# Three blocks of a modulation product moved behind the first half's state products, and u's read-back asked for ahead of the blocks' loads

## The chip, the cores and the metric

The kernel runs on one core of a Trainium2 chip, in float32. The metric is the device time of one execution in microseconds, as the median of several runs. TensorE multiplies, VectorE, ScalarE and GpSimd work element by element, and SyncE issues most of the DMAs, in one fixed order, waiting on semaphores where a buffer or an operand isn't ready.

## What is computed

One layer of a diffusion backbone on 256 latent tokens and 256 context tokens of width 1024, cut to what matters here:

```
mod_x = silu(c) @ w_mod + b_mod        # 1024 x 6144: shift1, scale1, gate1, shift2, scale2, gate2
mod_c = silu(c_ctx) @ w_mod + b_mod
hx = modulate(rmsnorm(x), shift1, scale1);   hc = the same of the context
ux = hx @ w_in;   uc = hc @ w_in[:, 512:]
states = bidirectional complex-diagonal scan of u[:, 512:], context first
ssm_x = gelu(C h + D u) * sigmoid(... @ w_glu)
pool_x = pooling mixer of ux[:, :512]
x = x + gate1 * (concat(pool_x, ssm_x) @ w_out)
h2 = modulate(rmsnorm(x), shift2, scale2)
x = x + gate2 * moe(h2)                # 32 experts, 1024 -> 512 -> 1024, top 2 of a routed group
out = rmsnorm(x)
```

## The kernel before

w_mod is used in three thirds of 2048 columns. The first third (shift1, scale1) is multiplied early. The second third (gate1, shift2) is loaded in eight blocks of 128 rows, 1 MB each, into three buffers in turn, and TensorE multiplies block k with the silu'd conditioning columns (`mod_chunk(1, k, 6)`, lines 503 and 511, all into PSUM bank 6). ScalarE then copies the sum to `modrow` (L983). The last third (scale2, gate2) is summed on VectorE (`mod_sum`) out of parts that `last_third` loads.

The scan is a matter of matrices. `u_ssm(q)` (L612) makes four groups of u. ScalarE evacuates each (L1015) and sends it to a scratch tensor in DRAM (L1018). SyncE reads it back in another layout, `U8`, in two halves of eight DMAs (L305), each half when both of its groups are out (`u_out0`, `u_out1`). `state_inputs(h)` (L644) multiplies the half's `U8` into four PSUM groups, n = 4h to 4h + 3. Group 2 also waits for `mo_ready`, since its bank holds operands of the tables that VectorE is making (`table`, L1179 and L1267). `turn_kernels` (L600) transposes the convolution kernels; ScalarE copies them and issues 15 Toeplitz copies (L1046, L1047), five ahead of the second half's states and ten behind them. VectorE scans the states, which ends in `hp_ready`.

`u_pool(t)` (L625) is the pooling half of the input projection, then come windows (L677), pooling weights (L683), the Toeplitz product (L692), the pooling part of the output projection (`mix_pool`, L699, which needs the `wo_pool` weights), the states' outputs (L715), the GLU (L737), the last third's row sums (L749, L750), the SSM part of the output projection (L790), the routing, and the loop over groups of four experts (L824 to L894).

TensorE's order and SyncE's order are both written out by hand. Every SyncE request stands behind the ones before it: w_mod blocks of the second third (L289), w_out in two parts (L315 `wo_ssm`, L319 `wo_pool`), the parts of the last third (L294), w_glu (L325), expert weights (L243, L250). A block's load waits on `mod_used`, a count of the blocks multiplied, for its buffer.

Of the kernel before, what the change touches and what calls it, by code (L numbers as in the profile page):

```python
# [58 lines left out]
def hybrid_block(nc, x, ctx, w_mod, columns, ssm_bc, b_mod_rows, w_in, w_out, w_pool, w_glu, w_router, b_router,  # L59
                 w_gate, w_up, w_down, g_final, consts, pool_consts, out):  # L60
    D = x.shape[2]
    KD = D // P
# [11 lines left out]
    with ExitStack() as stack:  # L74
# [5 lines left out]
        def S(name):  # L80
            if name not in sems:
                sems[name] = stack.enter_context(nc.semaphore(name))
            return sems[name]
# [181 lines left out]
        def _(sp):  # L265
# [35 lines left out]
            for h in range(2):  # L301
                sp.wait_ge(S(f"u_out{h}"), 16 * 2)
                at = slice(128 * h, 128 * h + 128)
                for s in range(L):
                    sp.dma_start(ra[SG * s:SG * (s + 1), 0:2048].rearrange("i (g n) -> i g n", g=8)[:, :, at],  # L305
                                 u_dram.rearrange("(g i) (s n) -> s i g n", g=8, s=L)[s][:, :, at]).then_inc(S(f"u8_in{h}"), 16)
                for k in range(3 + 3 * h, min(6 + 3 * h, KD)):
                    mod_chunk(1, k)
                if h == 0:
                    sp.wait_ge(S("mo_powers"), 1)  # L310
                    sp.wait_ge(S("pw_ready"), 1)
                    sp.dma_start(wpool, w_pool[0].rearrange("g c d -> c g d")).then_inc(S("wpool_in"), 16)
# [182 lines left out]
        def _(pe):  # L495
# [127 lines left out]
            def u_pool(t):  # L623
                for k in range(KD):
                    mm = pe.matmul(ps[:, t, :], hT[:, k, 256 + P * t:256 + P * t + P], WBp[:, k, :],  # L625
                                   start=(k == 0), stop=(k == KD - 1))
                mm.then_inc(S("u_pool_mm"), 1)
# [23 lines left out]
            pe.wait_ge(S("win_ssm_in"), 16)  # L651
            u_ssm(0)
            u_ssm(1)
            pe.wait_ge(S("ks_copy"), 1)
            for k in range(3):
                mod_chunk(1, k, 6)
            u_ssm(2)
            u_ssm(3)
            pe.wait_ge(S("st_copy"), 16)
            state_inputs(0)  # L660
            turn_kernels()
            for k in range(3, 6):
                mod_chunk(1, k, 6)
            state_inputs(1)
            for k in range(6, KD):
                mod_chunk(1, k, 6)
            pe.wait_ge(S("kt_ready"), 2)
            pe.wait_ge(S("win_pool_in"), 16)
            u_pool(0)
            u_pool(1)  # L670

            pe.wait_ge(S("pmat_in"), 16)
# [947 lines left out]
```

## Time and profile before

| | us |
|---|---|
| median of 3 runs | 660.44 |
| lowest, highest | 660.02, 662.47 |
| profiled execution | 657.66 |
| its span | 655.8 |
| TensorE busy | 589.1 (90%) |
| VectorE busy | 202.2 (31%) |
| ScalarE busy | 146.9 (22%) |

The page of the profile cuts the span into 40 slices of 16.4 us and gives the busy share of each engine, the clock granted to TensorE and what the DMA engines moved. Of the chain that ended last, 70% is TensorE and 24% DMA. The timeline gives merged instructions in order of time, with idle time ahead of them and what ended it.

### The profile page before, as it was taken

The numbers are of one execution on the slowest core, as the hardware profiler recorded it, in microseconds if no ns is written. First come the engines' busy times: TensorE is split into PE (matmuls) and PEld (weight loads), VectorE is DVE, ScalarE is ACT, GpSimd is POOL, SyncE is SP. The second block draws the span as 40 slices with busy tenths as digits, with TensorE's granted clock in tenths as the row PEclk, the third lists the DMA queues.
The fourth block names the chain that finished last, engine by engine and source line by source line (L and its number), as shares of the span: only waits on it lengthen the run. The fifth ranks groups of instructions, "written<-read, shape, count | busy, mean of one in ns | idle before, by whom it ended". The sixth has DMA issues, their size and how long they took to land.

```text
span 655.8 us, 9396 instructions
## 1 busy us (share of the span) xinstructions
PE 589.1 (90%) x3778; PEld 248.8 (38%) x3778; DVE 202.2 (31%) x434; ACT 146.9 (22%) x231; POOL 52.1 (8%) x99
## 2 busy tenths in 40 slices
PE   1999969999979997899799789979997997999995
PEld 0454544564543342334233323423342342334331
DVE  7999679968830020011001000200200010002003
ACT  8551321131232122102121301221022112012111
POOL 4994000000010000000000000000000000000000
PEclk9999979999999998999799989989998999899998
DMA  8994799998989999999999999999999999999951
GB/s 323 420 399 120 254 319 337 410 408 320 364 321 416 420 420 423 423 421 420 423 423 423 419 423 422 424 419 422 423 423 419 422 423 423 422 420 375 404 233 64
DMA packets 47463, 248.99 MB, mean 380 GB/s; under 512 B 8888, under 2 KB 11592, under 8 KB 21072
## 3 DMA queue, kind: packets, MB, share of 16 engines
q1 hardware_dynamic: 41224, 243.93, 91.6%
q10 hardware_dynamic: 5864, 3.68, 2.1%
q0 software_dynamic: 352, 1.07, 0.7%
q8 instruction: 15, 0.25, 0.2%
q14 instruction: 8, 0.07, 0.0%
HBM read 244.46 MB, written 2.11 MB: 376 GB/s over the span
## 4 chain that ended last, share of the span: by engine, by line
PE 70%; DMA 24%; DVE 2%; SPq 1%; issue 1%; ACT 1%; DVEq 0%; POOL 0%
PE ps L854 24%; DMA wts<-in_w_up 17%; PE ps L894 17%; PE ps L830 5%; PE ps L824 5%; PE ps L612 4%; DMA wts<-in_w_in 3%; PE ps L699 2%; PE ps L625 2%; PE ps L790 2%; DMA wts<-in_w_mod 2%; PE ps L870 1%; PE ps L737 1%; PE ps L511 1%; PE ps L644 1%
## 5 line engine op out<-in xcount | busy, mean ns | idle before, releaser
L854 PE MATMUL ps<-wts,ra 128*64 128x512 f32 x512 | 241.8, 625 | 34.2 <-DMA wts<-in_w_up 31.3
L855 PE MATMUL ps<-wts,ra 128*64 128x512 f32 x512 | 241.9, 626 | 0.0
L854 PEld LDWEIGHTS ps<-wts,ra 128*64 128x64 f32 x512 | 70.0, 143 | 179.6 <-issue 136.3
L894 PE MATMUL ps<-wts,ra 128*32 128x512 f32 x512 | 111.4, 593 | 0.0
L894 PE MATMUL ps<-rc,ra 128*32 128x512 f32 x512 | 111.4, 593 | 0.0
L1179 DVE TENSOR_TENSOR ra<-ra,ps 128x256 f32<-128x256 f32 x32 | 13.5, 421 | 267.9 <-ACT ra L1128 267.8
L1122 ACT COPY ra<-ps 128x512 f32<-128x512 f32 x32 | 33.6, 1050 | 208.9 <-PE ps L855 208.9
L855 PEld LDWEIGHTS ps<-wts,ra 128*64 128x64 f32 x512 | 70.0, 143 | 0.0
L894 PEld LDWEIGHTS ps<-wts,ra 128*32 128x32 f32 x512 | 29.1, 110 | 73.2 <-issue 73.2
L1179 DVE TENSOR_TENSOR cb<-ps,ra 128x512 f32<-128x512 f32 x32 | 22.1, 691 | 103.4 <-PE ps L894 103.4
L1117 ACT COPY ra<-ps 128x512 f32<-128x512 f32 x32 | 18.7, 585 | 133.2 <-PE ps L824 133.2
L483 POOL TENSOR_SCALAR small<-small 128x1 f32<-128x1 f32 x4 | 0.7, 186 | 473.4 <-ACT ra L1160 465.1
L824 PEld LDWEIGHTS ps<-cb,ra 128*128 128x128 f32 x256 | 29.8, 191 | 13.4 <-issue 6.5
L824 PE MATMUL ps<-cb,ra 128*128 128x128 f32 x256 | 32.8, 281 | 0.9 <-ACT ra L1111 0.9
L830 PE MATMUL ps<-cb 128*128 128x512 f32 x68 | 32.9, 606 | 0.0
L612 PE MATMUL ps<-ra,wts 128*128 128x512 f32 x64 | 29.4, 599 | 1.4 <-DMA wts<-in_w_in 1.0
L894 PEld LDWEIGHTS ps<-rc,ra 128*32 128x32 f32 x512 | 29.2, 110 | 0.0
L1179 DVE TENSOR_TENSOR cb<-cst,ut 128x256 f32<-128x256 f32 x16 | 6.7, 420 | 46.0 <-PE ps L824 44.8
L870 PEld LDWEIGHTS ps<-cst,ra 128*128 128x128 f32 x128 | 14.2, 141 | 17.2 <-issue 15.3
L511 PE MATMUL ps<-wts,sil 128*32 128x512 f32 x96 | 13.2, 637 | 7.7 <-DMA wts<-in_w_mod 7.7
L870 PE MATMUL ps<-cst,ra 128*128 128x128 f32 x128 | 18.8, 280 | 0.0
L830 PEld LDWEIGHTS ps<-cb 128*128 128x128 f32 x68 | 11.6, 190 | 15.5 <-issue 14.6
(228 smaller groups left out, 533.1 us busy)
## 6 DMA issues: line engine op xcount, KB each, us to landing
wts<-in_w_up SPq DMA_DIRECT2D x64, 1024.0 KB, 15.5
wts<-in_w_gate SPq DMA_DIRECT2D x64, 1024.0 KB, 13.4
wts<-in_w_down SPq DMA_DIRECT2D x30, 1024.0 KB, 9.8
rc<-in_w_down SPq DMA_DIRECT2D x30, 1024.0 KB, 12.5
wts<-in_w_mod SPq DMA_DIRECT2D x16, 1024.0 KB, 14.9
r<-in_w_mod SPq DMA_DIRECT2D x6, 1024.0 KB, 14.1
wts<-in_w_in SPq DMA_DIRECT2D x2, 2048.0 KB, 23.2
wts<-in_w_out SPq DMA_DIRECT2D x2, 2048.0 KB, 17.0
```

The source lines that it names most:

```text
L511: mm = pe.matmul(ps[32 * j:32 * j + 32, bank, :], silc[:, k, :], w[:, 512 * j:512 * j + 512], start=False, stop=(k == KD - 1))
L612: mm = pe.matmul(ps[:, 4 + q % 2, :], WBs[:, k, P * q:P * q + P], hT[:, k, :], start=(k == 0), stop=(k == KD - 1))
L625: mm = pe.matmul(ps[:, t, :], hT[:, k, 256 + P * t:256 + P * t + P], WBp[:, k, :], start=(k == 0), stop=(k == KD - 1))
L824: mm = pe.matmul(o, h2P[:, t, k, :], Pm[:, t], start=True, stop=True, skip_group_check=True)
L830: mm = pe.matmul(ps[:, 2 * t + h, :], PT[:, t, :], oS[:, 2 * h + t, :], start=False, stop=stop, skip_group_check=True)
L854: pe.matmul(ps[0:64, 4 + b, :], st, Wg[b][:, k, :], start=(k == 0), stop=(k == KD - 1))
L855: mm = pe.matmul(ps[64:128, 4 + b, :], st, Wu[b][:, k, :], start=(k == 0), stop=(k == KD - 1))
L870: mm = pe.transpose(ps[:, 6 + j % 2, P * f:P * f + P], gu[:, j % 2, P * f:P * f + P], ident)
L894: mm = pe.matmul(ps[32 * j:32 * j + 32, BANKS[n], :], hid[:, j, f, SLOTS * t:SLOTS * t + SLOTS], Wd[j][:, f, 512 * h:512 * h + 512], start ...
L1117: act.copy(xm[:, 2 * r:2 * r + 2], ps[:, GATHER[r], :].rearrange("p (k e s) -> p k e s", k=2, e=4)).then_inc(S("xm_ready"), 1)
L1122: act.copy(gu[:, j % 2, :].rearrange("p (f q) -> p q f", f=FC), ps[:, 4 + j % 2, :].rearrange("p (q f) -> p q f", f=FC)).then_inc(S("gu_co ...
L1179: return dve.tensor_tensor(o, a, b, op)
```

## The change

On SyncE, the loads of blocks 3 to 5 of the second third move from behind the first half's read-back to behind the second half's, together with 6 and 7. On TensorE, blocks 0 to 2 move from between u_ssm(1) and u_ssm(2) to behind the first half's states and the kernels' transposes; blocks 3 to 5 move behind the second half's states; blocks 6 and 7 move between u_pool(0) and u_pool(1).

```diff
                                  u_dram.rearrange("(g i) (s n) -> s i g n", g=8, s=L)[s][:, :, at]).then_inc(S(f"u8_in{h}"), 16)
-                for k in range(3 + 3 * h, min(6 + 3 * h, KD)):
+                for k in range(3 * h, KD * h):
                     mod_chunk(1, k)
...
             u_ssm(0)
             u_ssm(1)
-            pe.wait_ge(S("ks_copy"), 1)
-            for k in range(3):
-                mod_chunk(1, k, 6)
             u_ssm(2)
             u_ssm(3)
             pe.wait_ge(S("st_copy"), 16)
             state_inputs(0)
             turn_kernels()
-            for k in range(3, 6):
+            pe.wait_ge(S("ks_copy"), 1)
+            for k in range(3):
                 mod_chunk(1, k, 6)
             state_inputs(1)
-            for k in range(6, KD):
+            for k in range(3, 6):
                 mod_chunk(1, k, 6)
             pe.wait_ge(S("kt_ready"), 2)
             pe.wait_ge(S("win_pool_in"), 16)
             u_pool(0)
+            for k in range(6, KD):
+                mod_chunk(1, k, 6)
             u_pool(1)
```

TensorE behind `u_ssm(1)`, before: the bias (L503) and three blocks (L511, `r` and `wts` being the buffers) stand ahead of the two u groups that are left (L612).

```order
L612 MATMUL ps<-ra,wts 128x512 x2
L503 MATMUL ps<-mr,cst 32x512 [waits bmod_in,ks_copy]
L503 MATMUL ps<-mr,cst 32x512 x3
L511 MATMUL ps<-r,sil 32x512 [waits wmod_in2]
L511 MATMUL ps<-r,sil 32x512 x3
L511 MATMUL ps<-wts,sil 32x512 [waits wmod_in0]
L511 MATMUL ps<-wts,sil 32x512 x3
L511 MATMUL ps<-wts,sil 32x512 [waits wmod_in1]
L511 MATMUL ps<-wts,sil 32x512 x3
L612 MATMUL ps<-ra,wts 128x512 [waits u_ssm_ev]
L612 MATMUL ps<-ra,wts 128x512 x7
```

TensorE at the same place, after: u follows at once, and the first half's states (L644) behind it.

```order
L612 MATMUL ps<-ra,wts 128x512 x2
L612 MATMUL ps<-ra,wts 128x512 [waits u_ssm_ev]
L612 MATMUL ps<-ra,wts 128x512 x7
L612 MATMUL ps<-ra,wts 128x512 [waits u_ssm_ev]
L612 MATMUL ps<-ra,wts 128x512 x7
L644 MATMUL ps<-ra,wts 64x64 [waits u_ssm_ev,u8_in0,st_copy]
L644 MATMUL ps<-ra,wts 64x64 x15
L644 MATMUL ps<-ra,wts 64x64 [waits u_ssm_ev]
L644 MATMUL ps<-ra,wts 64x64 x15
L644 MATMUL ps<-ra,wts 64x64 [waits mo_ready]
L644 MATMUL ps<-ra,wts 64x64 x15
```

So the first half's states, their wait for `mo_ready` among them, come earlier by the bias and three blocks.

TensorE behind the last group of the second half's states, after: three blocks, u_pool(0), two blocks, u_pool(1). Before, only the two blocks of buffers 2 and 0 stood there, ahead of both u_pool.

```order
L644 MATMUL ps<-ra,wts 64x64 x15
L511 MATMUL ps<-r,sil 32x512 [waits wmod_in2]
L511 MATMUL ps<-r,sil 32x512 x3
L511 MATMUL ps<-wts,sil 32x512 [waits wmod_in0]
L511 MATMUL ps<-wts,sil 32x512 x3
L511 MATMUL ps<-wts,sil 32x512 [waits wmod_in1]
L511 MATMUL ps<-wts,sil 32x512 x3
L625 MATMUL ps<-wts,ra 128x512 [waits win_pool_in,kt_ready]
L625 MATMUL ps<-wts,ra 128x512 x7
L511 MATMUL ps<-r,sil 32x512 [waits wmod_in2]
L511 MATMUL ps<-r,sil 32x512 x3
```

The work of eight blocks is as before; five of them now stand behind the second half's states instead of two.

SyncE between the two read-backs, the difference (three block loads leave the place ahead of w_pool and the second read-back):

```order
 L305 DMA ra<-u_scratch 16x8x128 [waits u_out0]
 L305 DMA ra<-u_scratch 16x8x128 x7
-L289 DMA r<-in_w_mod 128x2048 [waits mod_used]
-L289 DMA wts<-in_w_mod 128x2048 [waits mod_used] x2
 L312 DMA lam<-in_w_pool 128x4x128 [waits pw_ready,mo_powers]
 L305 DMA ra<-u_scratch 16x8x128 [waits u_out1]
 L305 DMA ra<-u_scratch 16x8x128 x7
+L289 DMA r<-in_w_mod 128x2048 [waits mod_used]
+L289 DMA wts<-in_w_mod 128x2048 [waits mod_used] x2
 L289 DMA r<-in_w_mod 128x2048 [waits mod_used]
 L289 DMA wts<-in_w_mod 128x2048 [waits mod_used]
```

All five blocks, 3 to 7, are now asked for behind the second read-back, and w_out's two parts behind them.

## Rows read from the trace of the kernel before

**Rows 1.** Page, section 2: what the DMA engines moved, in 40 slices of 16.4 us

```profile
GB/s 323 420 399 120 254 319 337 410 408 320 364 321 416 420 420 423 423 421 420 423 423 423 419 423 422 424 419 422 423 423 419 422 423 423 422 420 375 404 233 64
```

**Rows 2.** Chain of waits: start us, us, what

```profile
77.01 4.30 DMA u_scratch<-ut
...
85.00 4.75 DMA ra<-u_scratch
...
119.73 7.06 PE ps L699 x16
...
185.83 0.64 PE ps L854
...
254.35 18.88 DMA wts<-in_w_up
```

**Rows 3.** TensorE timeline, 40 to 120 us: start us, us, instruction, idle before

```profile
58.60 1.06 PE L503 MATMUL ps<-mr,cst 1*32 1x512 f32 x8
...
62.30 14.00 PE L612 MATMUL ps<-ra,wts 128*128 128x512 f32 x32
76.23 3.95 PE L644 MATMUL ps<-ra,wts 128*64 128x64 f32 x128
80.11 1.09 PE L600 MATMUL ps<-cst,cb 128*128 128x128 f32 x8
...
89.79 6.32 PE L644 MATMUL ps<-ra,wts 128*64 128x64 f32 x128 [5.88 <-DMA ra<-u_scratch]
...
97.90 14.00 PE L625 MATMUL ps<-wts,ra 128*128 128x512 f32 x32
```

**Rows 4.** Windows of 1 us: length, busy per engine, TensorE's granted clock, DMA share, GB/s

```profile
88.00:89.00 1.00, 0.00 (x0) 0.00 (x0) 0.93 (x4) 0.00 (x0) 0.00 (x0) 0.62 1.25 246
...
95.00:96.00 1.00, 1.00 (x36) 0.98 (x32) 0.00 (x0) 0.77 (x2) 0.00 (x0) 0.97 1.04 410
```

**Rows 5.** VectorE timeline: last table, first gate sum, gated products

```profile
75.32 1.22 DVE L1267 SCALAR_TENSOR_TENSOR rc<-rc,ps 128x1024 f32<-128x1024 f32 x1
...
143.89 0.75 DVE L1387 TENSOR_SCALAR cb<-wts,sil 128x1024 f32<-128x1024 f32 x1
...
148.72 2.00 DVE L1179 TENSOR_TENSOR wts<-rc 128x256 f32<-128x256 f32 x4
```

**Rows 6.** SyncE: timeline row of a read-back; waits for expert weights' requests (in total, times, longest)

```profile
62.26 3.65 SPq L305 DMA_DIRECT2D ra<-u_scratch  x8
...
SPq L243 <- PE ps L855: 237.4, 60, 10.2
```

**Rows 7.** DMA queues (packets, MB, engine share): q10 over 84 to 88, q1 over 120 to 156

```profile
q10 hardware_dynamic: 356, 0.60, 73.3%
...
q1 hardware_dynamic: 3160, 14.86, 101.9%
```

**Rows 8.** One request each, issue start us, then its landing: wo_pool, blocks 3, 6, last gate's first

```profile
L319 SPq DMA_DIRECT2D wts<-in_w_out x1: 368/368/368, 96.2 to 96.2; - x1
...
DMA to landing us min/median/max: 18.8/18.8/18.8
...
L289 SPq DMA_DIRECT2D r<-in_w_mod x1: 428/428/428, 66.0 to 66.0; - x1
...
DMA to landing us min/median/max: 5.5/5.5/5.5
...
L289 SPq DMA_DIRECT2D r<-in_w_mod x1: 529/529/529, 85.7 to 85.7; - x1
...
DMA to landing us min/median/max: 6.5/6.5/6.5
...
L294 SPq DMA_DIRECT2D wts<-in_w_mod x1: 378/378/378, 128.3 to 128.3; - x1
...
DMA to landing us min/median/max: 13.4/13.4/13.4
```

**Rows 9.** TensorE timeline, 120 to 200 us: SSM part of the output projection

```profile
152.40 12.18 PE L790 MATMUL ps<-wts 128*128 128x512 f32 x28
```

## The prediction

> **What bounds the kernel now.** I read the chain of waits first, then the TensorE timeline of the stretch that the diff touches, then what the DMA queue does there. The second half of the kernel is the expert loop. Its passes wait for expert weights (such a step of the chain is 18.9 us long), and the slices of the page carry 420 GB/s from there to the end [rows 1, 2]. The requests for those weights wait for TensorE's own gate and up products [rows 6], so the stream cannot start before the loop does, at 185.83 [rows 2]. A microsecond won or lost ahead of 185.83 is a microsecond at the end. The change lies at 58 to 112 us, so the question is what it does to 185.83.
>
> In the stretch, TensorE multiplies three w_mod blocks at 58.60 to 62.30 while u of the last two groups is still owed. That u then goes out to DRAM and back (write 4.30, read back 4.75 behind its last issue), and TensorE stands idle for 5.88 us ahead of the second half's states at 89.79 [rows 2, 3]. The idle costs twice. The granted clock is 0.62 at 88 to 89 us and is back at 0.97 at 95 to 96, so it went from the 2.4 GHz level to the 1.2 GHz level after some 4.7 us of standing, and the 128 state matmuls behind it took 6.32 us where the same 128 of the first half took 3.95 [rows 3, 4]. From 97.9 on TensorE has work almost without a gap until it reaches the output projection at 119.73 [rows 2, 3].
>
> **The change on TensorE.** Bias and three blocks are worth 62.30 - 58.60 = 3.70 us; leaving them out there ends u_ssm(3) at 76.23 - 3.70 = 72.5. The first half's four state groups are 3.88 us (76.23 to 80.11), 0.97 each [rows 3]. Groups 0 and 1 run to 74.5. Group 2 waits for mo_ready, which VectorE gives behind a table that ends at 75.32 + 1.22 = 76.54 [rows 5]; before, TensorE came to that wait at 78.2 and never felt it. So 2.0 us of new idle, states done at 78.5, the kernels' transposes (1.03) at 79.6, bias and blocks 0 to 2 at 81.5, 82.4 and 83.3.
>
> u of the second half: evacuated and sent at 73.2, written by 77.5 if the write stays at 4.30, eight reads issued over 3.65 us [rows 6], landed at 85.5 if the last takes 4.75 again. No w_mod block moves beside it now, so it will be sooner; I take 83.3, no wait, with 85.5 as the late end. At full clock the states are then done at 87.2. If nothing else were in the way the gain would be 5.88 - 2.0 = 3.9 us of idle and 6.32 - 3.95 = 2.4 of clock, 6.3 in all.
>
> **What is late next: blocks 3 to 5.** SyncE asked for them at 66 us, in a stretch in which the DMA engines had room (254 GB/s in that slice) [rows 1, 8]. Now the requests stand behind the reads of u and each needs the buffer of block 0, 1 or 2, so they go out at 81.6 to 83.4. A block on an idle queue landed 5.5 us after its issue, so block 3 lands at 87.2. In a full queue q1 moved 14.86 MB in 36 us, 2.53 us for a block of 1.049 MB [rows 7, 8]. That gives 89.7 and 92.2 for blocks 4 and 5. Beside them run the Toeplitz copies that ScalarE issues: its first five took 73.3% of the engines over 84 to 88, 2.9 us, and some more at the edges, 3.7 at most [rows 7]. They start about 1.5 us sooner now (their releaser, the kernels' transposes, is that much earlier), so part of them is over before block 3's data come. I take 1.6 us, bounds 0 and 3.7. Block 5 lands at 93.8 (92.2 to 95.9), TensorE is through with it at 94.8, and has waited three times for about 1.6 us on the way.
>
> Then u_pool(0), 7.0 us (half of the 14.00), blocks 6 and 7 (1.9 together, asked for behind blocks 3 and 4, and landed 5 to 8 us behind block 5, under the 7.0), u_pool(1): 110.7, where before it ended at 111.9. TensorE would stand ready for the output projection at 119.73 - 1.2 = 118.5 (116.9 to 120.6).
>
> **The weights of the output projection.** wo_pool was asked for at 96.2 and landed 18.8 later, at 115.0, with 4.7 us to spare [rows 8]. The six MB between block 6 (85.7 + 6.5 = 92.2) and wo_pool took 22.8 us where a clear queue needs 15.2; the other 7.6 are the later ten Toeplitz copies and their small packets. Now the queue holds ten MB in a row: block 3 at 87.2 + 1.6, then four blocks, wo_ssm 2, the first gate part 1 and wo_pool 2, nine times 2.53 = 22.8, and the same 7.6: 119.2 (117.6 to 121.3). The issue gates don't break this row: each next request is released by a block that lands before the ones ahead of it are through. So the weights come 4.2 us later than before, eat the 4.7 to spare, and the projection starts at 119.2 to 119.4 where it started at 119.73: **-0.4 us** (-2.1 to +1.6). The gain of 6.3 is almost all taken back by 3 MB that used to move in a free stretch.
>
> hp_ready doesn't decide: before, TensorE came to it at 119.73 + 7.06 = 126.8 and went on at once; VectorE's work on the second half starts with its states, some 5 us sooner now, and TensorE comes at about 126.4. SyncE's waits for blocks 6 and 7 now stand in front of wglu's request, but that is released by u_pool(1), which is later on TensorE than both.
>
> **Behind it.** The queue stays 4.2 us late until it runs empty near 156 us. Of what lands in it, one thing is near its use: the first part of the last gate, 128.3 + 13.4 = 141.7, used by VectorE at 143.89 [rows 5, 8]. At 145.9 VectorE is 2.0 late, its four gated products start at 150.7 instead of 148.72 and end at 152.7. TensorE comes for them at 152.4 and takes 0.86 us for each where VectorE takes 0.5 [rows 5, 9], so it waits for none, but VectorE is a few tenths late for its next step. I put 0 to 0.6 on it, **+0.3**.
>
> **Sum** against the profiled execution's own 657.66 (span 655.8): -0.4 + 0.3 = -0.1, 657.6. The median of the runs shown is 660.44, 2.8 above that execution, so the same sum gives **660.3**. The bounds -2.1 and +2.2 give 658.3 and 662.6.
>
> **Rivals.**
> *The loads come in time (faster).* If the first five Toeplitz copies are through before block 3's data, block 5 lands at 92.2 and wo_pool at 117.6; TensorE is ready at 116.9. The projection starts 2.1 us sooner, VectorE's gate parts are only 2.6 us late: 658.3. For it: nothing moves at 80 to 82 us except those copies. Against: they were strung over 6 us before. To be over 0.5% faster (3.3 us) the ten later copies would have to cost less than 7.6 as well. Chance 0.21, of that 0.05 for more than 3.3.
> *The clock falls again (slower).* TensorE has bursts of 0.95 us between waits of 1.6 from 87 to 94. If that is enough for the 1.2 GHz level to be granted for as long as before (about 6.8 us, from the change inside 88 to 89 to the one inside 95 to 96 [rows 4]), it falls on u_pool(0) and half of it is lost, 3.4 us: ready at 121.9, +2.2 and 0.3 more behind, 662.9. It decides as soon as it costs over 0.7 us, since the weights are only that much later than TensorE. Against: the one fall in this stretch came after 4.7 us without a single matmul, and the gaps here are a third of that, 1.6 each. Chance 0.13. The Trainium skill speaks for it: "TensorE: Matmul & The Clock Gate", section on HAM oscillation, describes a kernel whose short bursts between DMA waits are thrown back to half clock at every wait. By that rule this rival would be the likeliest; but the waits it describes are 3 to 5 us long, and the trace agrees only for the long one.
> *The queue is later than I take it (slower).* All 3.7 us of Toeplitz work fall on the blocks: wo_pool lands at 121.3, +1.6; the gate part is 4.1 late, the products end near 154.8, and VectorE's next step carries 0.9 of it: +2.5, 662.9. It decides from a tax of 2.1 us on. Chance 0.13. The Trainium skill's "DMA: Bandwidth & Descriptors", rules for kernel authors, says to issue a DMA early and wait for it late; the change does the opposite for three blocks. By that rule alone one would expect the loss; the trace agrees in so far as slice 66 to 82 had room that is now unused [rows 1].
> *The idle isn't filled as the change says.* If u still lands at 85.5, the states end at 89.4, and block 5 at 93.8 is met later with less waiting. 94.8 stays. This falls together with the forecast.
>
> **How the numbers follow.** Forecast 0.50, loads in time 0.21, clock 0.13, late queue 0.13, anything else 0.03. The range takes in the rivals' times and about half a us at each end for the spread of the runs: 657.8 to 663.3. A measurement of this kernel can tell about 0.5%, 3.3 us. Over 3.3 faster: 0.05, and 0.01 of the rest. Over 3.3 slower: where the clock and the full tax come together (120.6 + 3.4 = 124.0, +4.3), 0.06, and 0.01 of the rest. Within: 0.87.
>
> **What the profile after would show.** Right: the 5.88 us idle ahead of the second states is gone or under 2 us; a new idle of about 2 us inside the first states, released by VectorE; states of the second half in some 4 us at clock 1.00; two or three idles ahead of blocks 3 to 5, released by DMA, 3 to 6 us in all; wo_pool landing at 118 to 121 with a wait of TensorE ahead of the output projection; expert loop starting within 1 us of 185.83. Wrong: no wait for blocks 3 to 5 (then the Toeplitz term is too big), clock below 1 anywhere in 88 to 103 (the second rival), or the loop starting more than 2 us away from 185.83 although wo_pool landed near 119.

## The result, and the profile after

| | before | after |
|---|---|---|
| median, us (20 runs each) | 660.82 | 664.04 |
| lowest, highest | 659.21, 665.3 | 659.87, 667.2 |
| profiled execution, its span | 657.66, 655.8 | 663.57, 661.8 |
| output projection's first matmul | 119.73 | 125.11 |
| expert loop's first matmul | 185.83 | 189.59 |

The ratio is 1.004 [1.0022, 1.0057]: the change makes the kernel slower by about 2.6 us (3.2 by the medians). That is outside the forecast's range, on the side of the slower rivals, and less than the 3.3 us that the prediction took as the least it could tell. Of all the executions below one, of experiment 2, was in a slower state (668.33 us); the ratios leave it out.

The DMA slices of the page after, to be laid beside [rows 1]:

```profile
GB/s 315 418 401 118 92 312 345 407 414 403 354 297 408 422 420 422 422 419 424 421 422 421 423 421 422 422 422 422 423 421 422 422 422 422 421 421 366 408 229 63
```

The fifth slice, 66 to 82 us, carried 254 GB/s before and carries 92 now. That is the 3 MB which moved out of it. The three slices behind it, into which the loads moved, carry the same as before within 3%: there was no room in them for more.

TensorE's timeline of the stretch (start us, us, instruction, idle before and what ended it), to be laid beside [rows 3]:

```profile
72.78 2.09 PE L644 MATMUL ps<-ra,wts 128*64 128x64 f32 x64
76.88 2.64 PE L644 MATMUL ps<-ra,wts 128*64 128x64 f32 x64 [2.01 <-DVEq L1302]
79.45 1.97 PE L600 MATMUL ps<-cst,cb 128*128 128x128 f32 x8
...
85.14 3.95 PE L644 MATMUL ps<-ra,wts 128*64 128x64 f32 x128
89.25 1.06 PE L511 MATMUL ps<-r,sil 128*32 128x512 f32 x8 [0.15 <-DMA r<-in_w_mod]
94.83 1.59 PE L511 MATMUL ps<-wts,sil 128*32 128x512 f32 x8 [4.52 <-DMA wts<-in_w_mod]
98.56 1.93 PE L511 MATMUL ps<-wts,sil 128*32 128x512 f32 x8 [2.13 <-DMA wts<-in_w_mod]
100.42 7.93 PE L625 MATMUL ps<-wts,ra 128*128 128x512 f32 x16
...
110.14 7.13 PE L625 MATMUL ps<-wts,ra 128*128 128x512 f32 x16
...
125.04 7.13 PE L699 MATMUL ps<-wts 128*128 128x512 f32 x16
```

The 5.88 us of idle ahead of the second half's states are gone, and these take 3.95 us instead of 6.32, as the change intends. In their place stand 2.01 us ahead of group 2 and 0.15, 4.52 and 2.13 ahead of blocks 3 to 5. The idle total is no smaller than before (8.8 us against 5.88). Two groups are also slow for their size: the 64 state matmuls at 76.88 take 2.64 us where the 64 ahead of them took 2.09, and the kernels' transposes (L600) 1.97 instead of 1.09.

The clock says why. Windows of 2 us of the kernel after: the column behind POOL is TensorE's granted clock, then DMA share and GB/s.

```profile
78.00:80.00 2.00, 2.00 (x37) 1.88 (x33) 0.00 (x0) 1.51 (x4) 0.00 (x0) 0.54 0.39 102
80.00:82.00 2.00, 2.00 (x15) 1.21 (x13) 1.29 (x4) 1.14 (x4) 0.00 (x0) 0.60 0.35 102
...
94.00:96.00 2.00, 1.17 (x8) 0.16 (x8) 1.93 (x7) 0.00 (x0) 0.00 (x0) 0.81 0.99 327
96.00:98.00 2.00, 0.42 (x4) 0.00 (x0) 1.97 (x7) 0.00 (x0) 0.00 (x0) 0.50 1.03 341
...
100.00:102.00 2.00, 2.00 (x6) 0.84 (x3) 1.93 (x9) 0.00 (x0) 0.00 (x0) 0.50 1.09 298
102.00:104.00 2.00, 2.00 (x6) 0.86 (x5) 1.83 (x11) 0.00 (x0) 0.00 (x0) 0.98 0.99 320
```

TensorE went from its 2.4 GHz level to the 1.2 GHz level soon behind the 2.01 us at mo_ready (the idle ends at 76.88, the clock is 1.00 up to 78), and again behind the 4.52 us ahead of block 4. It is at half speed over most of 78 to 82 and of 95 to 102.

SyncE's timeline shows the requests:

```profile
76.44 4.84 SPq L305 DMA_DIRECT2D ra<-u_scratch  x8
83.56 0.35 SPq L289 DMA_DIRECT2D r<-in_w_mod  x1
84.41 1.19 SPq L289 DMA_DIRECT2D wts<-in_w_mod  x2
```

| block | asked for | landed | forecast for the landing |
|---|---|---|---|
| 3 | 83.56 | 89.2 | 88.8 |
| 4 | 84.4 | 94.8 | 91.3 (89.7 + 1.6) |
| 5 | 85.3 | 98.5 | 93.8 |

The DMA queues over 84 to 88 and 92 to 96 us (packets, MB, share of the 16 engines); q1 carries SyncE's loads, q10 ScalarE's Toeplitz copies:

```profile
q1 hardware_dynamic: 126, 1.02, 84.4%
q10 hardware_dynamic: 132, 0.20, 16.1%
...
q1 hardware_dynamic: 149, 1.08, 80.4%
q10 hardware_dynamic: 147, 0.25, 20.4%
```

While the copies run, q1 brings 1.02 MB in 4 us, 0.26 MB/us, where [rows 7] has 0.41. All 15 copies were issued before block 5 had landed: five over 82.6 to 85.1, ten over 89.2 to 95.6.

The chain that ended last runs through the load of block 5, and not through wo_pool (start us, us, what):

```profile
85.27 13.24 DMA wts<-in_w_mod
98.56 1.93 PE ps L511 x8
...
125.11 7.06 PE ps L699 x16
```

wo_pool was asked for at 101.0 and landed 21.2 us later, at 122.2. That is later than forecast (119.2, at most 121.3), but 2.9 us ahead of its use. The load of block 5 and TensorE's work behind it decided.

### The profile page after: what moved, and what is told of

Same layout as the page of the kernel before. It is cut to its first block, busy times and chain, and to the rows that moved or that the text cites. A ratio compares the mean times of both kernels' runs of the same rounds, so it can differ in the third digit from the quotient of the medians.

```text
span 661.8 us, 9396 instructions
## 1 busy us (share of the span) xinstructions
PE 592.2 (89%) x3778; PEld 248.2 (38%) x3778; DVE 202.5 (31%) x434; ACT 147.0 (22%) x231; POOL 52.0 (8%) x99
## 3 DMA queue, kind: packets, MB, share of 16 engines
q10 hardware_dynamic: 5864, 3.68, 2.0%
q0 software_dynamic: 352, 1.07, 0.7%
## 4 chain that ended last, share of the span: by engine, by line
PE 63%; DMA 22%; DVE 11%; issue 1%; SPq 1%; ACT 0%; DVEq 0%; POOL 0%
PE ps L854 23%; DMA wts<-in_w_up 19%; PE ps L894 17%; PE ps L830 5%; PE ps L824 4%; DVE rc L1179 4%; DVE ps L1179 3%; PE ps L625 2%; PE ps L699 2%; PE ps L790 2%; DMA wts<-in_w_mod 2%; DMA cb<-in_ssm_bc 1%; PE ps L870 1%; PE ps L737 1%; PE ps L511 1%
## 5 line engine op out<-in xcount | busy, mean ns | idle before, releaser
L612 PE MATMUL ps<-ra,wts 128*128 128x512 f32 x64 | 29.1, 597 | 1.4 <-DMA wts<-in_w_in 1.0
L511 PE MATMUL ps<-wts,sil 128*32 128x512 f32 x96 | 14.8, 701 | 14.9 <-DMA wts<-in_w_mod 14.8
```

The source lines that it names most:

```text
L511: mm = pe.matmul(ps[32 * j:32 * j + 32, bank, :], silc[:, k, :], w[:, 512 * j:512 * j + 512], start=False, stop=(k == KD - 1))
L612: mm = pe.matmul(ps[:, 4 + q % 2, :], WBs[:, k, P * q:P * q + P], hT[:, k, :], start=(k == 0), stop=(k == KD - 1))
```

## The experiments

All are set against runs of the kernel before on the same chip. The medians of before were 660.92 (29 runs; experiments 1 to 4), 661.24 (23 runs; 5 to 8) and 660.67 (29 runs; 9 to 11). Times at which TensorE starts a group are those of its timeline, in which the projection starts at 119.66 in before and at 125.04 in after. Each kernel has one trace, so such a time is one execution's.

**1. Blocks behind u_pool.** The SyncE order of the change is kept, and TensorE has 7 us of other work while blocks 3 to 5 come. ScalarE's copy of the sum goes behind its two copies of u (those lines are left out here).

```diff
             state_inputs(1)
-            for k in range(3, 6):
-                mod_chunk(1, k, 6)
...
             u_pool(0)
-            for k in range(6, KD):
+            for k in range(3, 6):
                 mod_chunk(1, k, 6)
             u_pool(1)
+            for k in range(6, KD):
+                mod_chunk(1, k, 6)
```

> The changed kernel, but TensorE takes blocks 3 to 5 only behind u_pool(0) and blocks 6 and 7 behind u_pool(1) (ScalarE copies the sum and sends it behind its two copies of u). No load is asked for earlier than in the changed kernel. Theory A, the late loads of blocks 3 to 5 hold TensorE: its 6.8 us of waits ahead of u_pool(0) vanish, u_pool(0) starts near 89 instead of 100.4; what is late next is wo_pool, which landed at 122.2 in the changed kernel and still does at 120 to 124, so TensorE then waits for it and the output projection starts at 120 to 123 instead of 125.1: 660 to 663. Theory B, the queue behind block 5 doesn't matter and only TensorE's path did: the projection starts at 114, some 11 us sooner, 653. Theory C, it is the granted clock that was lost and not the blocks: the clock falls at the wait for mo_ready as before, and the time stays near 664.

Measured: 662.28, ratio 1.0012 [0.9985, 1.0039]. TensorE's timeline:

```profile
76.82 3.55 PE L644 MATMUL ps<-ra,wts 128*64 128x64 f32 x64 [2.26 <-DVEq L1301]
...
88.90 7.13 PE L625 MATMUL ps<-wts,ra 128*128 128x512 f32 x16
...
99.05 1.07 PE L511 MATMUL ps<-wts,sil 128*32 128x512 f32 x8 [1.16 <-DMA wts<-in_w_mod]
...
121.16 8.75 PE L699 MATMUL ps<-wts 128*128 128x512 f32 x16 [4.88 <-DMA wts<-in_w_out]
```

The three waits of 6.8 us shrink to 1.16, TensorE is ready for the projection at 116.3, and then it stands 4.88 us for wo_pool. So the late blocks are what puts the projection at 125 in after, and behind them the full queue holds this cure at 121. The clock falls again behind the 2.26 us at mo_ready (3.55 us for 64 matmuls) and behind the 4.88 us (8.75 us for the 16 matmuls of the projection, 7.13 in before).

**2. Blocks 0 to 2 inside the mo_ready wait.**

```diff
                     elif n == 2:
+                        pe.wait_ge(S("ks_copy"), 1)
+                        for k in range(3):
+                            mod_chunk(1, k, 6)
                         pe.wait_ge(S("mo_ready"), 1)
```

> The changed kernel with blocks 0 to 2 between the second and the third group of the first half's states, where TensorE stood idle for 2.0 us on mo_ready. The idle vanishes and the clock shouldn't fall at 78; blocks 0 to 2 end at 78 instead of 85, so that the loads of blocks 3 to 5 go out right behind u's read-back, at 81.3 instead of 83.6 to 86. Theory A: the blocks land about 2 us sooner, block 5 at 96, and the end comes 2 to 3 us sooner than in the changed kernel, 661 to 662. Theory C, clock: the same idle filled gives 1.6 us at full clock, and more if the later falls go too, 660 to 662; the two are told apart by the landings of blocks 4 and 5. If neither, 664.

Measured: 661.4, ratio 1.0004 [0.9981, 1.0028]. The 2.0 us idle is gone, the clock stays at 1.00 there, the requests go out at 80.9 instead of 83.6, block 5 is multiplied at 94.08 and the projection starts 4.5 us sooner than in after:

```profile
90.33 1.07 PE L511 MATMUL ps<-wts,sil 128*32 128x512 f32 x8 [1.46 <-DMA wts<-in_w_mod]
94.08 1.94 PE L511 MATMUL ps<-wts,sil 128*32 128x512 f32 x8 [2.68 <-DMA wts<-in_w_mod]
95.95 7.89 PE L625 MATMUL ps<-wts,ra 128*128 128x512 f32 x16
...
120.52 7.13 PE L699 MATMUL ps<-wts 128*128 128x512 f32 x16
```

Filling that one idle takes back the whole loss that can be measured, but no more: the time can't be told from before's. The late queue is still felt further on. VectorE waits for the last gate's first part, which it did not in before, and TensorE for the gated products behind it:

```profile
146.79 0.75 DVE L1387 TENSOR_SCALAR cb<-wts,sil 128x1024 f32<-128x1024 f32 x1 [3.58 <-DMA wts<-in_w_mod]
```

```profile
152.71 12.26 PE L790 MATMUL ps<-wts 128*128 128x512 f32 x28 [0.91 <-DVE wts L1179]
```

**3. All Toeplitz copies behind block 5.**

```diff
-            toeplitz(range(3))
             take_states(1)
-            toeplitz(range(3, L))
+            act.wait_ge(S("mod_used"), 14)
+            toeplitz(range(L))
```

> The changed kernel, but ScalarE issues all 15 Toeplitz copies behind block 5's product instead of five ahead of and ten behind the second half's states. Theory A1, the Toeplitz copies on the other queue take the engines from blocks 3 to 5: blocks 4 and 5 land 2.5 us apart, at 91.7 and 94.2 instead of 94.8 and 98.5, u_pool(0) starts at 95 instead of 100.4; the copies land by 118 and the projection starts near 120 to 121: 659 to 661. Theory A2, the blocks are late only because they are asked for late, and the copies cost them nothing: landings at 94.8 and 98.5 as before, 664 or more, since the copies themselves now are late.

Measured: 668.2, ratio 1.0092 [1.0059, 1.0126]. TensorE's timeline:

```profile
93.39 1.06 PE L511 MATMUL ps<-wts,sil 128*32 128x512 f32 x8 [2.68 <-DMA wts<-in_w_mod]
94.39 7.13 PE L625 MATMUL ps<-wts,ra 128*128 128x512 f32 x16
...
121.67 3.64 PE L692 MATMUL ps<-wts,ra 128*32 128x128 f32 x64 [5.28 <-DMA wts<-ra]
```

Blocks 3, 4 and 5 land 5.2, 7.3 and 10.2 us behind their requests; in after it was 5.6, 10.4 and 13.2. The copies cost block 5 **3.0 us**. The other 2.1 of the 5.1 by which block 5 is sooner here are the earlier request (83.16 against 85.27). Over 84 to 88 q1 brings 1.61 MB here, 1.02 in after. Even without copies block 5 came 3.7 us behind block 4, not 2.53. Over 90 to 94 us of this run q1 moved 1.25 MB, 0.31 MB/us, with no copies beside it: the rate of 0.41 [rows 7] was not reached here. The kernel as a whole loses, against 659 to 661 expected: the Toeplitz product now waits 5.28 us for its copies and runs at half clock behind that, so the projection starts at 125.24, as in after. What this run loses beyond after lies behind the projection (pauses and clock, see below).

**4. Useless matmuls in the waits.** Extra work on TensorE into PSUM banks that are overwritten later, nothing left out: two in front of the mo_ready wait, five ahead of block 4, two ahead of block 5.

```diff
+            def filler(n, bank):
+                for _ in range(n):
+                    pe.matmul(ps[:, bank, :], ident, cst[:, 0:512], start=True, stop=True)
...
                     elif n == 2:
+                        pe.wait_ge(S("ks_copy"), 1)
+                        filler(2, 6)
                         pe.wait_ge(S("mo_ready"), 1)
...
+            pe.wait_ge(S("kt_ready"), 2)
             mod_chunk(1, 3, 6)
+            filler(5, 0)
             mod_chunk(1, 4, 6)
+            filler(2, 0)
             mod_chunk(1, 5, 6)
```

> The changed kernel with matmuls of no use (128x512 of constants into a PSUM bank that is overwritten later) in its three waits: two ahead of the wait for mo_ready, five ahead of block 4, two ahead of block 5. They keep TensorE busy and change nothing else. Theory C, the granted clock is what was lost: it stays at 1.00 over 76 to 104, states and transposes of 76 to 82 take 1.6 us less, blocks 4, 5 and the start of u_pool(0) 2 us less: 660 to 661. Theory A, the loads: blocks 4 and 5 still land 11 and 14 us behind block 2, only what lies behind block 5 gains, about 1.5 to 2 us: 662 to 663.

Measured: 662.99, ratio 1.0025 [0.9998, 1.0052]. The clock is 1.00 from 76 to 173 us and the projection starts at 122.13:

```profile
97.32 1.07 PE L511 MATMUL ps<-wts,sil 128*32 128x512 f32 x8 [0.48 <-DMA wts<-in_w_mod]
98.31 7.13 PE L625 MATMUL ps<-wts,ra 128*128 128x512 f32 x16
```

So the two clock falls are worth 2.9 of the 5.4 us at the projection: 1.2 because blocks 3 to 5 are asked for and land sooner, 1.7 in the product of block 5 (1.93 to 1.07) and u_pool(0) (7.93 to 7.13). The median fits the 662 to 663 that the theory of the loads gave. It does not show the whole 2.9, and this execution lost more than that again at 173 to 181 (see below).

**5. Blocks 3 and 4 early, in space of their own.** On top of experiment 2, SyncE asks for blocks 3 and 4 once u_ssm is done, ahead of the second read-back, into 16 KB per partition that is free then. The lines that choose the buffers, and the later places of wo_ssm and of the last third's parts, are left out here.

```diff
             for h in range(2):
+                if h == 1:
+                    sp.wait_ge(S("u_ssm_mm"), 4)
+                    mod_chunk(1, 3)
+                    mod_chunk(1, 4)
                 sp.wait_ge(S(f"u_out{h}"), 16 * 2)
```

> As the run with blocks 0 to 2 in the wait for mo_ready, but blocks 3 and 4 get buffers of their own, the space of w_in's SSM columns, which is free when u_ssm(3) is done. They are asked for at 72.5, ahead of the second read-back, in a stretch in which the DMA engines have almost nothing to do; block 5 is asked for behind the read-back, blocks 6 and 7 right behind it. wo_ssm waits for blocks 3 and 4, the parts of the last third for block 7. Theory A, the 3 MB that used to move in a free stretch are what was lost: blocks 3 and 4 land at 78 to 80, TensorE waits for none of the five, u_pool(0) starts near 90, wo_pool lands near 115, and the output projection starts at 115 to 116 against 119.7 of the kernel before: 657 to 658, faster than before. Theory D, once TensorE is early something else (VectorE's scan, the last third's parts) takes the place: 660 to 661.

Measured: 664.54, ratio 1.0056 [1.0035, 1.0076], the opposite of what I expected. The last u group's write, issued at 76.5, is only through at 85.5, and TensorE stands 9.55 us:

```profile
94.10 6.33 PE L657 MATMUL ps<-ra,wts 128*64 128x64 f32 x128 [9.55 <-DMA ra<-u_scratch]
```

That write took 2.9 us in after, 4.30 in before and some 9 us here: 2 MB of blocks stood ahead of its small packets. (This execution was 3.2 us late at the end of u_ssm already; the 9.55 us of idle are not part of that.)

**6. Blocks 6 and 7 between the two u_pool, alone.** The kernel before with only this.

```diff
-            for k in range(6, KD):
-                mod_chunk(1, k, 6)
...
             u_pool(0)
+            for k in range(6, KD):
+                mod_chunk(1, k, 6)
             u_pool(1)
```

> The kernel before with only the last part of the change: blocks 6 and 7 between u_pool(0) and u_pool(1). Loads and everything ahead of the second half's states as before. Both blocks land (92 and 96) before the states end, so TensorE does the same work in another order. All theories of mine: no difference, 660 to 661, and the output projection at 119.7. If this part alone cost something (ScalarE's copy of the sum, the last third's parts that are asked for behind it), it would show as 1 us or more and would have to be taken off the loads' account.

Measured: 660.56, ratio 0.9998 [0.9979, 1.0017], the projection at 119.70. This part of the change costs and brings nothing.

**7. SyncE's old order.** Experiment 2 with blocks 3 to 5 asked for ahead of the second read-back again.

```diff
-                for k in range(3 * h, KD * h):
+                for k in range(3 + 3 * h, min(6 + 3 * h, KD)):
```

> As the run with blocks 0 to 2 in the wait for mo_ready (all other places of TensorE as in the changed kernel), but with SyncE's order of before: blocks 3 to 5 are asked for ahead of the second read-back. Blocks 0 to 2 end at 76.4 to 78.2 there, so the requests go out then, 5 us sooner than behind the read-back, and the read-back's eight requests only from 78.3 on instead of 76.1, beside 3 MB of blocks. Theory A, the place of the requests on SyncE is what costs: blocks 3 to 5 land at 82, 85 and 88 and hold nobody; u lands at 85 to 88 instead of 82.9, the states start 2 to 5 us later, and the two about cancel on TensorE, while wo_pool lands 3 us sooner: 659.5 to 660.5. Rival: the read-back is the longer wait, the idle ahead of the states is back with its fall of the clock, 661 to 662.

Measured: 671.29, ratio 1.0164 [1.0139, 1.0189]. SyncE's and TensorE's timelines:

```profile
80.09 8.32 SPq L305 DMA_DIRECT2D ra<-u_scratch  x8
```

```profile
94.58 5.66 PE L647 MATMUL ps<-ra,wts 128*64 128x64 f32 x128 [13.21 <-DMA ra<-u_scratch]
```

Beside three block loads the eight requests of a read-back take 8.32 us to issue, not 3.65 [rows 6], and TensorE waits 13.2 us. Both readings that I had set out (659.5 to 662) missed this. With blocks 0 to 2 multiplied this late, asking for u first is right, and worth 10 us: 8.0 at the projection (128.52 against 120.52 in experiment 2), the rest behind it. What made the old SyncE order good was the old TensorE order, which let blocks 3 to 5 go at 66 us.

**8. The kernel before with filler.** Five useless matmuls in its wait for u; nothing is left out.

```diff
+            pe.wait_ge(S("kt_ready"), 2)
+            filler(5, 0)
             state_inputs(1)
```

> The kernel before with five matmuls of no use (128x512 of constants into a PSUM bank that is overwritten later) in its 5.88 us wait for u, nothing else changed. Theory C, the clock: it stays at 1.00 over 84 to 96, the second half's states take 3.95 instead of 6.32 us, and the output projection starts at 117.4 instead of 119.7 (wo_pool has landed at 115.0 by then): 658 to 659. Theory D, what follows is held by the queue or VectorE: 660 to 661.

Measured: 660.01, ratio 0.9986 [0.997, 1.0002].

```profile
91.18 3.95 PE L648 MATMUL ps<-ra,wts 128*64 128x64 f32 x128 [1.45 <-DMA ra<-u_scratch]
...
97.48 1.07 PE L511 MATMUL ps<-wts,sil 128*32 128x512 f32 x8 [1.36 <-DMA wts<-in_w_mod]
```

The states take 3.95 us, the 2.4 us of clock are won, and then TensorE waits 1.36 us for block 7, which it did not in before. The projection starts at 120.24. This execution came to the stretch 1.3 us late (its bias of the second third starts at 59.92, before's at 58.60), so from there to the projection it is 60.3 us against 61.1: 0.7 of the 2.4 us arrive. Of the prize that the change is after, little is there to be won, because the loads behind it are nearly as late. That the median is 1.2 us lower is not shown to be more than noise (the interval reaches 1.0002).

**9. Output weights first.** TensorE's orders of 1 and 2 together; on SyncE wo_pool ahead of blocks 6 and 7, wo_ssm behind the last third's first part, and the first expert weights later.

```diff
-            sp.wait_ge(S("u_ssm_mm"), 4)
+            sp.wait_ge(S("s_mm"), 8)
+            sp.dma_start(wo_pool, w_out_v[:, 0:4, :]).then_inc(S("wo_pool_in"), 16)
+            for k in range(6, KD):
+                mod_chunk(1, k)
+            sp.wait_ge(S("mod_used"), 14)
+            last_third(0, 0)
             sp.dma_start(wo_ssm, w_out_v[:, 4:8, :]).then_inc(S("wo_ssm_in"), 16)
-            sp.wait_ge(S("mod_used"), 14)
-            last_third(0, 0)
-            sp.wait_ge(S("s_mm"), 8)
-            sp.dma_start(wo_pool, w_out_v[:, 0:4, :]).then_inc(S("wo_pool_in"), 16)
```

> The version that the runs so far point to. TensorE: blocks 0 to 2 in the wait for mo_ready, blocks 3 to 5 behind u_pool(0), blocks 6 and 7 behind u_pool(1). SyncE: behind the second read-back blocks 3 to 5, then wo_pool at once, then blocks 6 and 7, the first part of the last third, wo_ssm; the first expert's up and second down weights go behind the last third's third part and x instead of ahead of them. The theory (TensorE waits for what stands ahead in the queue, never for its own work): blocks 3 to 5 are there behind u_pool(0), wo_pool lands near 103 to 106, TensorE starts the pooling part of the output projection at 112 to 114 and then waits for VectorE's scan, which ends at 121 to 122, where the kernel before came there at 126.8: 655 to 657, faster than before by 4 to 5 us. Rival: the expert weights that now stand later in the queue are late for the loop, or the ten megabytes ahead of the gates' parts still hold VectorE: 660 or more.

Measured: 662.01, ratio 1.001 [0.9987, 1.0033], as the rival had it (660 or more). The projection starts at 120.91, not at 112 to 114. TensorE was through u_pool(1) at 104.7, and then:

```profile
107.77 1.91 PE L511 MATMUL ps<-r,sil 128*32 128x512 f32 x8 [3.06 <-DMA r<-in_w_mod]
111.33 1.93 PE L511 MATMUL ps<-wts,sil 128*32 128x512 f32 x8 [1.64 <-DMA wts<-in_w_mod]
```

The wait moved from wo_pool to blocks 6 and 7. VectorE shows one more bound behind all this: its copies of the Toeplitz operands wait for the last copy, in this kernel as in after (2.79 us there):

```profile
114.88 0.63 DVE L1366 COPY ra<-wts 128x256 f32<-128x256 f32 x2 [2.95 <-DMA wts<-ra]
```

The scan that follows ends at 125. The pooling part of the projection takes 7.1 us and TensorE needs the scan behind it, so a projection sooner than about 118 would have met VectorE.

**10. The later ten Toeplitz copies behind block 5.** The first five stay.

```diff
             take_states(1)
+            act.wait_ge(S("mod_used"), 14)
             toeplitz(range(3, L))
```

> The changed kernel, with only the later ten Toeplitz copies issued behind block 5's product; the first five stay where they are. It tells which of the two sets delays the blocks. My prediction charged the first five (1.6 us) and put the ten behind block 5. If the ten are what hit blocks 4 and 5, these land 7.5 and 10.5 us behind their issue, as in the run with all fifteen behind (7.3 and 10.2), instead of 10.4 and 13.2, and block 5 is there at 95 to 96. If it was the first five, block 5 stays near 98. The end: the ten copies are late for the Toeplitz product as all fifteen were there, so 665 to 668 either way.

Measured: 663.08, ratio 1.0033 [1.0011, 1.0054].

```profile
76.30 2.09 PE L644 MATMUL ps<-ra,wts 128*64 128x64 f32 x64 [1.67 <-DVEq L1303]
...
92.71 1.94 PE L511 MATMUL ps<-wts,sil 128*32 128x512 f32 x8 [4.14 <-DMA wts<-in_w_mod]
95.63 1.93 PE L511 MATMUL ps<-wts,sil 128*32 128x512 f32 x8 [0.99 <-DMA wts<-in_w_mod]
97.49 9.00 PE L625 MATMUL ps<-wts,ra 128*128 128x512 f32 x16
```

Block 4 lands 10.4 us behind its request, exactly as in after, and block 5 12.4, where it was 13.2 with all copies and 10.2 with none. Of the 3.0 us the first five copies cost 2.2 and the ten 0.8. (Block 5 is multiplied at 95.6, the time that I had expected if the ten were to blame, but because its request went out 2.1 us sooner than in after; only the time from request to landing tells the two apart.) Here the idle at mo_ready is 1.67 us and the clock holds (2.09 us for 64 matmuls); it falls in block 4's wait of 4.14 us. The end was not the 665 to 668 I had expected from a late Toeplitz product: the projection starts at 123.18. It falls once more further on, with TensorE at work all the time (1.91 to 2.00 us busy in each 2 us from 170 to 180). These eight matmuls take 3.68 us in before:

```profile
174.28 6.42 PE L761 MATMUL ps<-rc,cst 128*128 128x512 f32 x8
```

**11. Both cures.** Experiment 2 and useless matmuls ahead of blocks 4 (two) and 5 (three); nothing is left out.

```diff
             mod_chunk(1, 3, 6)
+            filler(2, 0)
             mod_chunk(1, 4, 6)
+            filler(3, 0)
             mod_chunk(1, 5, 6)
```

> The run with blocks 0 to 2 in the wait for mo_ready (661.4, 0.5 us over before), with two and three matmuls of no use ahead of blocks 4 and 5 as well, so that the clock doesn't fall at 94.6 as it did there. It separates what is left of the clock from what is left of the loads. Clock: u_pool(0) takes 7.13 instead of 7.89 us and block 5's product 1.07 instead of 1.94, the output projection starts at 119.0 instead of 120.5, 660 to 661. Loads: TensorE's waits for blocks 4 and 5 are filled, not shorter, and block 5 still lands at 94: nothing below 660.

Measured: 661.81, ratio 1.0015 [0.9997, 1.0033]. The clock is 1.00 up to 181 us, and:

```profile
119.58 7.13 PE L707 MATMUL ps<-wts 128*128 128x512 f32 x16 [0.20 <-DMA wts<-in_w_out]
```

With no clock lost anywhere the projection starts where it starts in before, and wo_pool now is the last to come. That is the balance that the prediction had forecast for the change itself.

## Why the prediction was wrong

**Right.** The idle ahead of the second states went, and they took 3.95 us at full clock. The new wait for mo_ready was 2.01 us (forecast 2.0). u came back in time. Three waits stand ahead of blocks 3 to 5, though longer than forecast (6.8 us; forecast 3 to 6). VectorE waited for its gate part, 1.25 and 0.41 us (forecast 2.0), and TensorE felt nothing of it. Moving blocks 6 and 7 cost nothing (experiment 6). Two of the signs of being wrong that the prediction named came true: the clock was below 1 in 88 to 103, and the loop started 3.8 us from 185.83.

**The step that failed: "Block 5 lands at 93.8 (92.2 to 95.9)".** It landed at 98.5, 4.7 late. Three terms of it were too small, and they add up to it:

| term | forecast | measured | from |
|---|---|---|---|
| request of block 5 | 83.4 | 85.3 (+1.9) | SyncE's timeline |
| Toeplitz tax on block 5 | 1.6 (0 to 3.7) | 3.0 (+1.4) | experiment 3 |
| request to landing without copies | 8.8 (83.4 to 92.2) | 10.2 (+1.4) | experiment 3 |

The first is mostly the clock. I had counted the 2.0 us at mo_ready as idle only, and wrote that short gaps would not bring a fall since "the one fall in this stretch came after 4.7 us without a single matmul". (That reading was off too: the idle began at 89.79 - 5.88 = 83.9, and a mean clock of 0.62 over 88 to 89 puts the fall at 88.2, 4.3 us later.) In the profiled execution of after, the fall came behind 2.01 us. The two state groups behind it took 0.55 us more, the transposes 0.88 and the bias 0.09, 1.5 in all; 0.3 is mo_ready itself, which came at 76.88 and not at 76.54. The requests, which wait for the buffers of blocks 0 to 2, went out 2 us late. This is a stall whose price is paid on another engine. The second is a choice inside a range: the trace had 3.7 as the upper end, and I took 1.6 because part of the copies would be over in time. They weren't: the three issued from 84 us on landed 7.4 to 10.8 us behind their issue, where the same three had taken 3.8 to 4.5 in before. And the price is not their own share of the engines' time (16.1%): beside 0.05 MB/us of q10, q1 fell from 0.40 (experiment 3) to 0.26 MB/us. For the third I used 2.53 us a block, the rate of a queue that had long been full [rows 7]; without copies block 5 still came 3.7 us behind block 4. Why the queue was slower there stays open.

**The clock rival and the late-queue rival came together.** Behind the landing of block 5 the clock cost 0.9 us in its product and 0.8 in u_pool(0). 4.7 + 0.9 + 0.8 = 6.4, and the forecast's 118.5 for TensorE becomes 124.9 (measured 125.0). I had put 0.06 on the two together costing more than 3.3 us, as if one came without the other. They are not independent: a later block makes a longer wait, behind which the clock can fall, and the lower clock behind mo_ready makes a later request. The price of the clock came out near (3.4 us forecast, 2.9 in experiment 4), but that is luck: I had put all of it on u_pool(0), where 0.8 fell; 0.9 fell on block 5's product, and the rest reached the projection by way of the later requests. The rule of the Trainium skill that I had set aside, "TensorE: Matmul & The Clock Gate", section on HAM oscillation, was the better guide: short bursts between DMA waits are thrown back to half clock. The trace after agrees for the wait of 4.52 us ahead of block 4. The 2.01 us at mo_ready are shorter than any wait that the section describes, and there the measurement goes further than the page.

The length of an idle does not decide by itself. Experiments 2 and 3 both wait 2.68 us for block 5: in 2 its product takes 1.94 us and u_pool(0) 7.89, in 3 they take 1.06 and 7.13, at full clock. Ahead of the loop TensorE stands 2.88 us in before and in after; the clock stays at 1.00 in before and falls in after. 1.67 us in experiment 10 left it at 1.00.

**"The weights come at 119.2, and the projection with them."** wo_pool landed at 122.2, 7.2 us later than before (forecast 4.2). From block 5 to wo_pool it was 23.7 us (forecast 25.4), so that stretch was 1.7 shorter than forecast, against 4.7 of lateness ahead of it. The weights were not the bound in after; they were in experiments 1, 7 and 11.

**From 5.4 to 3.8 us, and to 2.6.** The projection starts 5.4 us later than in before, the loop 3.8. Between the projection and the GLU 1.6 us came back. In before, two pauses stand in this stretch, which nothing in the profile but "issue" explains; with them L715 and L727 take 1.6 us more. They are absent in after:

```profile
132.21 1.07 PE L715 MATMUL ps<-rc,ra 64*32 64x128 f32 x54 [0.76 <-issue]
...
138.13 0.60 PE L727 MATMUL ps<-cst,rc 128*128 128x128 f32 x4 [0.36 <-issue]
```

(These lines are of before.) Pauses of 0.4 to 1.8 us stand there in before and in experiments 3, 4, 6, 8 and 11, and none in after and in 1, 2, 5, 7, 9 and 10. Their cause stays open, and with one trace a kernel it isn't shown that they belong to the kernel and not to the execution. So it isn't known how much of the step from 3.8 to 2.6 they are. In the profiled execution of after the loop's first pass ran at half clock for some 3 us (a window of 2 us):

```profile
192.00:194.00 2.00, 2.00 (x8) 0.64 (x6) 0.00 (x0) 0.00 (x0) 0.00 (x0) 0.50 0.67 274
```

The first pass takes 5.28 us here and 3.59 in before, so 1.7 of the 6.0 us by which the two spans differ are this fall. Experiments 6, 8 and 9 have such a fall at 186 to 190 too, and before has not; experiments 6 and 8 keep before's order of the loads, so the fall does not need the change. The spread of after (659.87 to 667.2) goes with the clock: the mean granted clock of the four fastest executions is 0.967 to 0.970, that of the four slowest 0.958 to 0.961. Where in these the clock fell is not known.

**What the rest comes to.** Of the 5.4 us at the projection, 4.5 go when blocks 0 to 2 fill the mo_ready wait (experiment 2: no fall there, requests sooner). The last 0.9 go with the clock behind blocks 4 and 5 (experiment 11). Nothing goes clearly below before's 119.7, since wo_pool, blocks 6 and 7 (experiment 9) and VectorE's scan stand within 2 us of one another there. No version of this order beat the kernel before.

The projection is not the whole story. First matmuls in one execution of each:

| | projection | GLU | loop | GLU to loop |
|---|---|---|---|---|
| before | 119.66 | 141.14 | 185.83 | 44.7 |
| after | 125.04 | 144.89 | 189.59 | 44.7 |
| experiment 2 | 120.52 | 140.37 | 187.97 | 47.6 |
| 4 | 122.13 | 143.51 | 191.62 | 48.1 |
| 8 | 120.24 | 142.26 | 188.60 | 46.3 |
| 9 | 120.91 | 140.76 | 185.47 | 44.7 |
| 10 | 123.18 | 143.03 | 191.05 | 48.0 |
| 11 | 119.58 | 141.35 | 186.18 | 44.8 |

Where the last column is above 44.8, the clock fell somewhere in 172 to 186 us with at most 0.1 us of TensorE idle ahead of it, and cost 1.7 us (experiments 2 and 8) or 3.4 (4 and 10; about as much in 3 and 7). In experiment 2, 0.9 us more is the wait for the gated products. The prediction had nothing for such a fall, and before and after have none, so it does not bear on the forecast. It does make a single execution's span a poor measure of a change worth 2 us.

## What to carry to other kernels

A load that moves out of a stretch in which the DMA engines have room into a full one is paid for where it is used next; price it by the order of the queue, the small copies of other queues included, and not by the bytes. An idle of 2 us on TensorE cost 1.5 us more in clock here, and where requests wait for what TensorE does behind it, the lateness is passed on to the loads. Existing work put into the new idle (experiment 2) repaired what the move had broken, but removing a stall can be worth little when the next three things are as late: ask first, as experiment 8 did, what the kernel gains if the stall is simply filled.

## What the runs showed of the hardware

- TensorE's granted clock fell to the 1.2 GHz level behind idles of 2.01 us (after) and 2.26 us (experiment 1), and stayed at 2.4 GHz behind 1.67 us (experiment 10). Behind 2.68 us it fell in experiment 2 and stayed in 3; behind 2.88 us it fell in after and stayed in before. Length alone doesn't tell.
- It also fell with TensorE at work: in experiment 10 over 172 to 180 us, busy 2.00 us of each 2, at a cost of 3.4 us.
- A write of 256 KB of u to DRAM in small packets took 2.9 us with no block beside it (after), 4.30 beside the end of the block loads (before), and 9.0 behind two blocks of 1 MB (experiment 5).
- Eight read-back requests took SyncE 3.65 us to issue in the first half, 4.1 to 5.0 in the other second halves, and 8.32 behind three block loads (experiment 7): the lateness falls on the engine that issues, and not only on the data.
- Copies within SBUF at 0.05 MB/us took 0.14 MB/us from the loads beside them (q1 over 84 to 88 us: 1.02 MB in after, 1.61 in experiment 3).
